# Input product of the second layer in seven block products, with its context columns first

## The reference, cut to what matters

```python
for layer in range(DEPTH):                              # 2 layers
    u  = _modulate(_rmsnorm(h,  norm1[layer]), sh1, sc1)      # 1024 latent tokens x 1024
    uc = _modulate(_rmsnorm(hc, norm1[layer]), csh1, csc1)    # 256 context tokens x 1024
    ...                                                 # layer 0: pooling and Fourier mixer
    # layer 1: u @ w_in and uc @ w_in, w_in is 1024 x 2560
    q, k, v, rkv, wl, al, gl = _split_sizes(u @ w_in, CD_SIZES)
    q_c, k_c, v_c, rkv_c, wl_c, al_c, gl_c = _split_sizes(uc @ w_in, CD_SIZES)
    ...                                                 # window attention, RWKV scans, output product
    h = h + gt2 * _conv_ffn(_modulate(_rmsnorm(h, norm2[layer]), sh2, sc2), *ffn)
```

## Time and profile before

| | us |
|---|---|
| median of 3 runs | 3197.09 (3195.32 to 3197.19) |
| the profiled execution | 3190.3 |
| its span, first to last instruction | 3188.5 |
| TensorE busy | 2957.6 (93%), mean granted clock 0.968 |
| VectorE busy | 2004.6 (63%) |
| GpSimd busy | 1240.6 (39%) |
| ScalarE busy | 1176.9 (37%) |

### The profile page before, as it was taken

The page is one execution under the profiler, slowest core; times in us unless marked ns, Lnnn a source line. Parts: engine busy times, 40 slices in busy tenths (PEclk is TensorE's granted clock), DMA queues, the critical chain, the costliest instruction groups (busy, mean ns, idle before and its releaser), DMA issues. The chain is left out here.

```text
span 3188.5 us, 67120 instructions
## 1 busy us (share of the span) xinstructions
PE 2957.6 (93%) x28494; PEld 2423.1 (76%) x28494; DVE 2004.6 (63%) x2838; ACT 1176.9 (37%) x2200; POOL 1240.6 (39%) x813
## 2 busy tenths in 40 slices
PE   6998999999999999899989888999979799999999
PEld 4655899977777777678867677777867688888887
DVE  4523389678877787702246667777746666666666
ACT  4011155433323323311146566666622433233232
POOL 3212033576667666333211100000004566666664
PEclk9998999999999999899989999999989899999999
DMA  6430045532323332122211011111012112111112
GB/s 238 147 129 34 20 148 177 165 106 87 118 93 99 106 112 86 48 88 84 90 58 53 21 33 31 31 34 32 23 49 83 40 40 67 40 53 66 40 53 79
DMA packets 135913, 247.35 MB, mean 78 GB/s; under 512 B 9537, under 2 KB 97985, under 8 KB 135490
## 3 DMA queue, kind: packets, MB, share of 16 engines
q1 hardware_dynamic: 97314, 193.92, 18.2%
q10 hardware_dynamic: 38304, 49.16, 4.5%
HBM read 221.15 MB, written 21.89 MB: 76 GB/s over the span
## 5 line engine op out<-in xcount | busy, mean ns | idle before, releaser
L1353 POOL TENSOR_TENSOR f_w_lo<-h,f_w_hi 128x512 fp32r<-128x512 f32 x92 | 138.9, 1518 | 150.4 <-ACT f_w_hi L1561 150.4
L3931 POOL TENSOR_TENSOR rw_inv_k<-rw_ss_k,rw_expo 128x4 f32<-128x4 f32 x20 | 20.2, 1008 | 441.1 <-ACT rw_ss_k L4234 441.1
L1429 PE MATMUL ps<-u_hi,f_w_hi 128*128 128x512 f32 x440 | 173.5, 394 | 9.1 <-DVE f_value L1674 4.3
L2209 POOL TENSOR_TENSOR f_w_lo<-f_u_hi_raw,f_w_hi 128x512 fp32r<-128x512 f32 x86 | 129.9, 1521 | 117.4 <-ACT f_w_hi L2457 117.4
L1429 PE MATMUL ps<-u_lo,f_w_hi 128*128 128x512 f32 x440 | 172.8, 393 | 0.0
L1429 PE MATMUL ps<-u_hi,f_w_lo 128*128 128x512 f32 x440 | 172.7, 392 | 0.0
L2209 POOL TENSOR_TENSOR f_w_lo<-f_w_raw,f_w_hi 128x512 fp32r<-128x512 f32 x84 | 127.3, 1523 | 99.1 <-ACT f_w_hi L2457 99.1
L1353 POOL TENSOR_TENSOR f_w_lo<-f_w_raw,f_w_hi 128x512 fp32r<-128x512 f32 x84 | 126.8, 1517 | 96.8 <-ACT f_w_hi L1561 96.8
L167 PE MATMUL ps<-u_hi,w_hi 128*128 128x512 f32 x552 | 145.2, 369 | 6.5 <-ACT cd_stage L1027 6.5
L2240 POOL TENSOR_TENSOR c_lo<-c_raw,c_hi 128x1024 fp32r<-128x1024 f32 x24 | 63.8, 2660 | 217.0 <-ACT c_hi L2419 217.0
L2339 PE MATMUL ps<-u_hi,f_w_hi 128*128 128x512 f32 x352 | 137.8, 391 | 10.4 <-DVE f_value L2591 10.4
(11 more groups left out here) (525 smaller groups left out, 9473.0 us busy)
## 6 DMA issues: line engine op xcount, KB each, us to landing
c_raw<-in_ffn SPq DMA_DIRECT2D x66, 512.0 KB, 3.5
f_w_raw<-in_ffn SPq DMA_DIRECT2D x64, 512.0 KB, 4.2
h<-in_ada_rows ACTq DMA_DIRECT2D x64, 512.0 KB, 3.8
h<-in_ffn SPq DMA_DIRECT2D x34, 512.0 KB, 4.6
f_u_hi_raw<-in_ffn SPq DMA_DIRECT2D x32, 512.0 KB, 4.7
ada_ring_s<-in_ada SPq DMA_DIRECT2D x22, 512.0 KB, 3.3
w_raw<-in_cd_in SPq DMA_DIRECT2D x20, 512.0 KB, 4.2
z_scratch<-cd_stage ACTq DMA_DIRECT2D x15, 640.0 KB, 5.4
```

Of the source, the lines that this page charges most:

```text
L1353: pool.tensor_tensor(two(w_lo[n % RING]), source(x), two(w_hi[n % RING]), ALU.subtract).then_inc(w_split, 1)
L1429: mm = pe.matmul(o, wt, xt, start=t in OPENS and j == 0 and i == 0, stop=j == HK - 1 and i == 2, skip_group_check=t not in OPENS)
L2209: pool.tensor_tensor(two(w_lo[n % RING][:, :]), source(x), two(w_hi[n % RING][:, :]), ALU.subtract).then_inc(w_split, 1)
L3931: pool.tensor_tensor(R.inv[:, :], R.ss[:, :], R.expo[:, :], ALU.pow).then_inc(inv_done, 1)
```

## The change

1. The 64 dots are spread in another way (`dot_places`). An up tile whose predecessor's gate work stands in its way (tiles 1, 2, 4, 6, ... 20 and 21) has one dot, after C12. The others ("alone": 0, 3, 5, ... 19) have one at their start and one after U3, some a third; a down step has three (after m = 0, 3 and 6), down 9 and the end step none.
2. In down 9 the banks go round in three sets instead of four, and DVE makes the gains at its start. The norm of the context columns (`CtxNorm`) goes into this step: squares on ACT, sums, root, scaling, high and low part. TensorE's order gets the norm's sums after m = 4 and its spread after m = 5.
3. The end step's first half takes its tiles in the order 6, 7, 2, 3, 0, 1, 4, 5. The squares of the latents are summed by POOL instead of DVE.
4. `InProduct` becomes `InHalves`: first the 15 weight tiles 4 to 18 on the 256 context columns (24 matmuls each), then all 20 tiles on the 1024 latents in 10 pairs (`PAIRS`), each pair with seven products of 12 matmuls of 512 columns, like an up tile. Beside the context tiles DVE makes the low part of two weight tiles in three, the taps, the norm of the first token half and the sums T1 to T4 for four j in four quarters each (56 instructions). The first products of pairs 0 and 1 are laid among the last context tiles; P7, P6, P5 of pair 0 and P7 of pair 1 run j by j.

```diff
@@ dots: where they stand
+    def alone(n):
+        return n == 0 or (n >= 3 and n % 2 == 1 and n < FT - 1)
+    def dot_places(kind, n):
+        if kind == "down":
+            return ("m0", "m3", "m6") if n < G - 2 else ()
+        if kind == "end":
+            return ()
+        if not alone(n):
+            return ("C12",)
+        return ("start", "U3") + (("C12",) if n == 0 else ("C21",) if n % 4 == 3 and n < 16 else ())
@@ down 9 and the end step on TensorE
     def down_banks(g, m):
-        return (first_set(g) + m // 2) % 2, 2 * (m % 2)
+        return ((0, 0), (1, 0), (1, 2))[m % 3] if g == G - 2 else ((1 + m // 2) % 2, 2 * (m % 2))
...
+                    turn = 3 if g == G - 2 else 4
-                    if m < 4:
+                    if m < turn:
...
                     else:
-                        pe.wait_ge(added, KT * g + m - 3)
+                        pe.wait_ge(added, KT * g + m - turn + 1)
...
+                    if g == G - 2 and m == 4:
+                        nxt.ctx.pe_sums(pe)
+                    if g == G - 2 and m == 5:
+                        nxt.ctx.pe_spread(pe)
...
-                for m in range(KT):
+                pe.wait_ge(act_ready, 2 * g + 1)
+                for m in (6, 7, 2, 3, 0, 1, 4, 5):
                     pe.wait_ge(w_split, NTH["end", g, (m // 4, 0)] + 1)
@@ down 9 on DVE
+                    if not late:
+                        rows.dve_finish(dve)
                     for m in range(KT):
                         add(n, m)
+                        dot(f"m{m}")
+                        if not late and m == 3:
+                            nxt.ctx.dve_accs(dve)
...
@@ down 9 on ACT
+                if (kind, n) == ("down", G - 2):
+                    if t == 3:
+                        nxt.ctx.act_squares(act)
+                    if t == 5:
+                        nxt.ctx.act_root(act)
+                    if t >= 6:
+                        for k in range(4 * (t - 6), 4 * (t - 6) + 4):
+                            nxt.ctx.act_hi(act, k)
@@ class InHalves, ACT: context tile n
+        for n in range(last + 1):
+            if n == 1:
+                norm.act_root(act, 1)
+            if n:
+                self.ctx_store(act, n - 1)
+            if n == last:
+                keep(0)
+            self.ctx_evict(act, n)
+            if n + 3 <= last:
+                self.c_high(act, n + 3)
+            self.act_item(act, n)
+            if last - 2 <= n < last:
+                high(n - last + 2)
@@ class InHalves, POOL
+        for c in range(2):
+            for m in range(1, KT):
+                norm.pool_acc(pool, c, m)
+                if (c, m) == (1, 3):
+                    c_low(0)
@@ class InHalves, DVE: context tile n
+            if self.conv(m):
+                dve.wait_ge(self.c_centre, self.c_taps_before(n) + 1)
+                conv_taps(dve, K, own, self.c_st[:, n % 4, :], self.c_bank(n), ...)
+            if n + 3 <= last and self.c_by_dve(n + 3):
+                c_low(n + 3)
+            self.dve_item(dve, n)
@@ class InHalves, TensorE
+        self.pe_product(pe, 0, P1)
+        self.pe_ctx(pe, len(self.CTX_TILES) - 1)
+        self.pe_product(pe, 0, P2)
+        self.pe_product(pe, 1, P1)
+        self.pe_product(pe, 1, P2)
+        for p, t in early[4:8]:
+            self.pe_before(pe, p, t)
```

More of the change, by code:

```diff
@@ L1793, in __init__, with three, place_sums, like_t4 @@
         self.b22 = [[x[:, j + HK, late] for j in range(HK)] for x in of]
+    def three(self, name, hi, lo):
+        x = [self.K.place(f"{self.TAG}_{name}_{y}", [P, HK, 512], dt, at=at) for y, dt, at in (
+            ("hi", F32R, hi), ("lo", F32R, lo), ("full", F32, lo))]
+        return [[y[:, j, :] for j in range(HK)] for y in x]
+    def place_sums(self, K):
+        return [self.three(name, at, at + 8192) for name, at in (
+            ("t2", K.w_at), ("t3", K.w_at + 16384), ("t4", K.s_at + 24576))]
+    def like_t4(self, x):
+        return x
     def dve_last(self, dve):
@@ L1808, in dve_sums @@
             if j == 0:
[L1809 to L1810 removed]
+                dve.wait_ge(self.spread, self.LATE + 1)
+                dve.wait_ge(self.lo_dve, self.LATE * KT)
             if j >= 2:
@@ new lines, with place_sums, like_t4, pool_acc @@
+class MergedNorm(ThreeWayNorm):
+    CHUNKS = [(0, 512, 0), (512, 512, 0)]
+    LATE = 1
+    TAG = "mn"
+    def place_sums(self, K):
+        hi, lo = K.s_at + 24576, K.s_at + 32768
+        t2 = self.three("t2", hi, lo)
+        t3 = self.three("t3", K.w_at + 8192, K.w_at + 24576)
+        gap = slice(SEQ, NT)
+        t4 = [[x[:, 2 * j:2 * j + 2, gap] for j in range(HK)] for x in (K.uhi, K.ulo, self.u_full)]
+        return t2, t3, t4
+    def like_t4(self, x):
+        return x.rearrange("p (a b) -> p a b", a=2)
+    def pool_acc(self, pool, c, m):
+        self.dve_acc(pool, c, m)
@@ L2502, in _ @@
                 kind, n, t = x
-                a, b = dots_in(kind, n)
+                if due is not None:
+                    rows.act_silu(act, due)
+                    due = None
                 if kind == "up":
@@ L2643, in _ @@
                         rounded(pending)
+                    dot("start")
                     merge(n, U2)
@@ L2647, in _ @@
                         low(pending)
-                    rows.dve_dot(dve, a)
+                    dot("U3")
                     merge(n, C22)
                     merge(n, C21)
+                    dot("C21")
                     taps(n, 1)
                     merge(n, C12)
-                    rows.dve_dot(dve, b)
+                    dot("C12")
                     taps(n, 0)
```

833 lines of the change are left out of this document (611 added, 222 removed).

## The result

The changed kernel takes 3214.6 us (median of 9 runs, 3198.2 to 3227.2) where the kernel before takes 3196.9 beside it: a ratio of 1.0053, 95% interval 1.0032 to 1.0073. It is 0.5% slower, forecast was 0.4% faster, and it lies above the stated range of 3156 to 3204. Its profiled execution took 3217.4 us, span 3215.6, 27 us more than that of before; the medians differ by 17.6.

The account below looks back on a forecast made before the run. TensorE's order was taken as the path, with DVE second where it waits. Dots -14, down 9 +17.5, end step and pairs -19, tail +2 sum to -13.5 us from 3197.1: 3183.6, rounded 3183; range 3156 to 3204.

Parts of the forecast that it names:

- The dots: Up tiles before down 9: new places of the row dots change the time by -14 us, bounds -8 and -20.
- The wait of about 1.0 goes, since the dot goes: Second up tile of each of eight middle groups: TensorE's wait of about 1.0 us for C22 disappears.
- The wait for U3 (1.1 each) mostly stays: Eight middle groups: the U3 wait of 1.1 us each remains, except some 0.4 us that is gained.
- rival C: Input product's pairs: bound by POOL, 32 us more if its instructions average 2.1 us, total 3216 us; chance 0.14.
- A third dot behind C21 costs 0.4: Up tiles with a third dot: it costs 0.4 us in each of 4 tiles, 1.6 us in all.
- The 5 us forecast for tiles 1, 2, 20 and 21: Outer up tiles: 5 us come off their waits, the longest (2.3 us) and with slow clock behind them.
- Down 9: From its first matmul to the end step's: in effect 39.6 us instead of 22.1, loss 17.5, bounds 10 and 22.
- The 3.2 for m = 3: In down 9: with three bank sets m = 3 waits for add 0 until 11.5 us, losing 3.2 us.
- End step to last product: From the end step's start to the last matmul's end: 310.6 us against 329.6, pairs 0 and 1 ending at 156.
- blocking: Between end step and group of four: DVE's list takes 10 us more through POOL instructions on SBUF operands.
- The tail: Behind the last matmul, to the next phase: 7.2 us instead of 5.2, with C12, tanh and copy, a store.
- Rival D: Up tiles: U3 and C22 form one chain, another instruction becomes late, only 3 of 14 us gained, 3194; chance 0.20.

Follow-up runs that it names:

- second pair of profiles: Kernel before and changed kernel, both unchanged, each run once more for a second profile: 3190.6 us for before; 3213.6 us for the changed kernel, ratio 1.0062.

## Why the prediction was wrong, point by point

Against the sum, by the first pair of profiles: the dots came out 27.6 us worse than forecast, down 9 3.1 better than its place of 37.6, the end step to the last product 8.9 worse, the tail as forecast.

**The dots, -14 forecast, +13.6 and +20.5 in two traces, +14.6 as a kernel: this step failed.** Its parts:
- "The wait of about 1.0 goes, since the dot goes" was right: no C22 wait is left. But it was counted as gain while the other wait of the pair was held fixed.
- "The wait for U3 (1.1 each) mostly stays" was wrong: counted in the same way it became 1.9 to 2.5 (1.7 to 2.3 of idle time), so the pair of waits cost as much as before or more. I had checked the start dot against DVE's list alone ("the start dots fit in the time in which DVE waits for P6") and not against POOL, though the earlier trace rows, which I used for rival C, show the coupling. (I read the two there as ended together; they end 0.56 us apart, as in the rows of the weight sums above.) In the runs without the start dot, or with ACT's scaling ahead of the cast, the U3 wait, so counted, is 0.6 to 1.1 and a group takes 61.0 to 62.1: for these groups my -1.0 each was right.
- "A third dot behind C21 costs 0.4" was mis-sized: 1 us a group in the changed kernel, 2.5 to 4 where no start dot hides it. I had taken the figure of a dot that lies beside ACT's scaling; this one stands ahead of the taps with its whole length, waits for its own load, and holds up ACT's issue of the next.
- Behind a wait of 1.8 or more can come some 1.5 us at half the clock, which no wait of 0.9 brought in any of these runs. The sum had no such term for waits that grow; it is 7.5 and 13.5 us of the 13.6 and 20.5.
- The 5 us forecast for tiles 1, 2, 20 and 21 did not come: up to down 0 it took 3 to 5 us more, and the stretch with the last three tiles gained 0.3 (86.8 to 86.5).

**Down 9, 37.6 forecast, 34.5 measured.** The two larger waits were right: 4.2 for the context sums (4.9 forecast), 4.1 ahead of the end step's first matmul (4.6). The 3.2 for m = 3 was 0.3, because the gains took 0.7 us in place of 3.0: I had read their cost from a place where something else lay between them. That the end step waits only for its ring slot, and that this is an accident of the operands' order, the run with the other order shows.

**End step to last product, 310.6 forecast, 319.5 measured.** The pairs took 19.04 each, as forecast (19.07), and rival C was wrong: POOL's 82 instructions in the eight pairs took 122.0 us, 1.49 each, under the 1.73 at which it would decide. The miss lies ahead of the group of four (126 forecast, 136.7 measured); the 2 us allowed for the eight pairs were not needed. DVE's list was the right thing to look at. The profile names POOL's low part as the last thing that TensorE waits for, but that waits for ACT, and ACT for DVE:

```profile
1444.59 0.62 ACT L1680 CAST mn_t_hi<-mn_t_full 128x512 fp32r<-128x512 f32 x1 [6.66 <-DVE mn_t_full L1657]
...
1446.41 1.80 POOL L1962 TENSOR_TENSOR in_w_lo<-in_s,in_w_hi 128x512 fp32r<-128x512 f32 x1 [3.00 <-ACT in_w_hi L2183]
```

Two of its terms were short. The list leads from 34.1 us behind the end step's start, not from 29 (context tile 1 started at 37.6 instead of 32.8). And blocking, put at 10, is 20.3, if one adds up by how much each of DVE's 104 instructions from there on exceeds the shortest of its kind; they overlap by some 6 in all. The work itself, 72.2 so counted, and DVE's idle time, 13.3, were near the forecast's 73 and 11. Six instructions in the last norm item alone took 1.64 to 1.75 instead of 0.69, and taking POOL's three sums away gave 3 us back.

**The tail** was right: 9.05 instead of 6.95, +2.1.

**What was not in the sum:** the attention, +0.8 to +4.9 by the granted clock. With it the traces add up: in the order of the table, and last the rest of the kernel, in the second pair of profiles 20.5 + 12.4 - 8.1 + 2.1 + 0.8 - 0.9 make 26.8, beside 25.6 of the spans (the first up tile starts 1.2 earlier in that one).

Rival D named the right place, with too small an effect: it had the C22 gain turn into another wait, not the chain grow.

## What to carry to other kernels

An instruction put into an engine's idle time is free only if the engine with which it takes turns has idle time there too; ask what else runs in that gap, what it is about to hand over, and what is queued behind that hand-over on a third engine. When two waits of one chain stand one behind the other, removing the second is worth nothing if the first grows, so cost them as one. A wait that has grown can cost twice, once as a wait and once as slower clock behind it, so look at what the same trace shows behind its longer waits.

## What the runs showed of the hardware

- A 128x1024 dot on DVE took 1.21 to 1.23 us alone and up to 2.37 beside POOL; a 128x512 instruction 0.69 and 1.75; POOL's 128x512 subtraction 1.29 and up to 1.8.
- U3 waits of 1.9 us were followed by the full clock in one group and by 0.76 in another of the same execution; behind those of 0.9 the clock never fell.
- Ten us of unchanged attention code, TensorE busy in all of it, ran at a granted clock of 0.90 and 0.86 in the two executions in which the phase took 199.6 and 199.7 us, and of 0.67 in the four others read there, of both kernels, in which it took 203.4 to 204.5.
